# A streaming encoder layer: stick-breaking attention by running sums of logarithms, and by scanned products of sigmoids

## What is computed

```python
def sb_block(q, k, v, q_start):
    z = jnp.einsum('bqhd,bkhd->bhqk', q, k) * scale
    vis = s[None, :] < t[:, None]
    log_keep = jnp.where(vis, jax.nn.log_sigmoid(-z), 0.0)
    later = lax.cumsum(log_keep, axis=3, reverse=True) - log_keep
    w = jnp.where(vis, jnp.exp(jax.nn.log_sigmoid(z) + later), 0.0)
    return jnp.einsum('bhqk,bkhd->bqhd', w, v)

u = a_val * jax.nn.sigmoid(a_gate)
a_out = jax.nn.silu(layernorm(causal_dwconv(concat([conv_hist, u]), conv_w, conv_b), ln_g, ln_b))
b_out = head_rmsnorm(stick_breaking(q, k_all, v_all, q_start), g_sb)
x = x + jnp.concatenate([a_out, b_out], axis=-1) @ w_out
```

## Time and profile before

| | us |
|---|---|
| runs | 595.35, 593.17, 595.15 |
| median | 595.15 |
| the profiled execution, its span from first to last instruction | 594.1 |
| PE busy | 542.8 (91%) |
| DVE busy | 289.6 (49%) |
| ACT busy | 166.8 (28%) |
| GpSimd busy | 105.8 (18%) |

### The profile page before, as it was taken

How to read it: one execution, slowest core, us unless ns; L and a number is a source line. 1 busy time by engine, 2 the same in 40 slices (tenths; PEclk the granted TensorE clock), 3 DMA queues, 4 the chain that set the end, 5 groups by cost and what they waited for, 6 DMA issues and landing times.

```text
span 594.1 us, 7819 instructions
## 1 busy us (share of the span) xinstructions
PE 542.8 (91%) x3097; PEld 330.3 (56%) x3098; DVE 289.6 (49%) x500; ACT 166.8 (28%) x280; POOL 105.8 (18%) x134
## 2 busy tenths in 40 slices
PE   6999999999999999799999799999999878888994
PEld 5779999998766644344554663444443323333331
DVE  2862999998868557362464852111112110011147
ACT  4513123222766776462210201111111111101113
POOL 3100000313431342300101121112112111011003
PEclk9999999999999999799999689999999999889998
DMA  8804745302403600049752879999999999999995
GB/s 294 223 2 148 239 145 172 114 1 57 165 19 89 255 0 1 0 117 421 278 213 88 302 265 400 424 423 424 424 425 417 428 423 422 417 423 421 412 365 171
DMA packets 44763, 148.93 MB, mean 251 GB/s; under 512 B 7124, under 2 KB 23532, under 8 KB 36279
## 3 DMA queue, kind: packets, MB, share of 16 engines
q1 hardware_dynamic: 40263, 139.63, 61.0%
q0 software_dynamic: 4464, 8.80, 3.9%
HBM read 136.29 MB, written 19.59 MB: 262 GB/s over the span
## 4 chain that ended last, share of the span: by engine, by line
PE 62%; DMA 19%; DVE 7%; ACT 4%; SPq 3%; issue 3%; POOL 2%; DVEq 0%; POOLq 0%; ACTq 0%
PE ps L983 17%; DMA big<-in_w_expert_out 12%; PE ps L1211 9%; PE ps L1398 8%; PE ps L1423 5%; DMA cw<-h_dram,low 4%; PE ps L948 3%; PE ps L1095 2%; SPq L642 2%; PE ps L1092 2%; PE ps L1379 2%; DMA y_dram<-cw,low 1%; DVE big L1935 1%; PE ps L1054 1%; PE ps L936 1%
## 5 line engine op out<-in xcount | busy, mean ns | idle before, releaser
L1857 DVE SCALAR_TENSOR_TENSOR big<-low,cwt,big 128x590 f32<-128x590 f32 x120 | 94.2, 841 | 0.4
L2233 DVE TENSOR_TENSOR low<-low,ps 128x256 f32<-128x256 f32 x16 | 6.7, 422 | 172.3 <-ACT low L1706 172.3
L1398 PE MATMUL ps<-big,low 128*64 128x512 f32 x320 | 85.0, 593 | 3.5 <-issue 2.3
L983 PE MATMUL ps<-cw_r 128*128 128x280 f32 x256 | 72.3, 292 | 0.0
L983 PE MATMUL ps<-low_r,cw_r 128*128 128x280 f32 x256 | 72.2, 292 | 0.0
L983 PE MATMUL ps<-cw_r,big_r 128*128 128x280 f32 x256 | 72.1, 291 | 0.0
L1423 PE MATMUL ps<-big,low 128*64 128x512 f32 x160 | 47.0, 630 | 11.7 <-DMA big<-in_w_expert_out 4.8
L1211 PE MATMUL ps<-cw,low 128*128 128x512 f32 x128 | 56.5, 594 | 0.0
L1398 PEld LDWEIGHTS ps<-big,low 128*64 128x64 f32 x320 | 29.8, 137 | 45.7 <-issue 45.7
L983 PEld LDWEIGHTS ps<-cw_r 128*128 128x128 f32 x256 | 47.2, 188 | 0.4 <-issue 0.4
L983 PEld LDWEIGHTS ps<-cw_r,big_r 128*128 128x128 f32 x256 | 47.3, 188 | 0.0
(11 more groups left out here) (285 smaller groups left out, 849.1 us busy)
## 6 DMA issues: line engine op xcount, KB each, us to landing
big<-in_w_expert_in SPq DMA_DIRECT2D x16, 2048.0 KB, 19.8
big<-in_w_expert_out SPq DMA_DIRECT2D x20, 1024.0 KB, 24.3
big<-in_w_in SPq DMA_DIRECT2D x20, 512.0 KB, 5.7
low<-in_w_expert_out SPq DMA_DIRECT2D x8, 1024.0 KB, 30.9
low<-in_w_expert_in SPq DMA_DIRECT2D x4, 2048.0 KB, 23.1
cw<-in_w_expert_in SPq DMA_DIRECT2D x4, 2048.0 KB, 26.8
low<-in_w_expert_in SPq DMA_DIRECT2D x4, 1536.0 KB
big<-in_w_expert_in SPq DMA_DIRECT2D x6, 1024.0 KB, 32.2
```

The lines of the kernel that those rows point to most:

```text
L983: return pe.matmul(ps[:, proj_bank(j) + half, 0:PROJ], w[:, k, :], h[:, k, cols], start=first, stop=last, skip_group_check=True)
L1398: mm = pe.matmul(ps[TILE * half:TILE * half + TILE, gu_bank(g), :], xt[:, k, TILE * half:TILE * half + TILE], wi_at(2 * g + half, k), star ...
L1857: ins = dve.scalar_tensor_tensor(conv[:, i, :], u[:, i, j:j + CW], cwt[:, i, j:j + 1], conv[:, i, :], ALU.mult, ALU.add)
```

## The change

**Attention after.** The list `order` has 24 entries, 21 of them steps, in groups: the four head pairs of query block 0 (128 keys), the few-query units (32 own keys and 512 others for the last prompt positions; 32 own and twice 512 cached keys for the sample), then query blocks 1, 2 and 3 with 256, 384 and 512 keys; three entries that turn the new keys for their output stand between. Queries lie on partitions, keys on columns, and a step holds two heads. Per step:

- PE makes the scores (`scores`). ACT makes two sigmoids of them, of -z (`keeps`) and of z (`betas`), both into SBUF. DVE scans each head's kept fractions from the last key backwards (`running_products`, tensor_tensor_scan, one instruction per head), with both operands the same SBUF tile.
- GpSimd multiplies the betas with the products shifted by one (`weights`), both in SBUF.
- PE turns the weights (`turn_weights`, three entries later), ACT copies them (`copy_weights`), and PE multiplies them with the values (`weigh`, four entries later). A step's score banks come free with `betas` of the step before last.

A group's outputs are copied and squared by ACT (`outputs`), reduced by DVE (`head_means`), rooted by GpSimd, scaled by DVE (`heads_normed`), turned by PE (`turn_out`) and put in place by DVE (`outputs_in`), five to nine entries after the group's end. `weigh` of the first step of a group from block 1 on waits until the group two before is in place.

**The convolution and the LayerNorm.** The first fifteen entries hold two taps each, the later ones none. The LayerNorm as a whole stands behind the attention: mean and variance are eight products each (before: two each, after sums on GpSimd), squares are on ACT. The output projection of chunks 0, 1 and 2 over the attention's channels (`LATE[0:4]`) stands ahead of the mean.

SyncE now waits for the attention's last output ahead of one more weight load, and stores the new keys in three groups. Later stages keep their instructions. The core of the diff:

```diff
-TAPS_STEP = (1, 2, 2, 1, 2, 2, 1, 2, 2, 1, 3, 2, 2, 1, 2, 1, 2, 2, 0, 0, 0, 0, 3)
-MEAN_AT = 26
-LAG = 4
+TAPS_STEP = (2,) * 15
+TURN_LAG, SUM_LAG, OUT_LAG = 3, 4, 5
+MEANS_LAG, ROOT_LAG, NORM_LAG, IN_LAG = 6, 7, 8, 9
...
+        groups = [many(0), few(1, 512, 0, 512) + few(0, S0, 32, PAST), many(1), many(2), many(3)]
+        CHUNK_OF = (0, 4, 1, 2, 3)
+        order = groups[0] + [dict(ko=0)] + groups[1] + [dict(ko=1)] + groups[2] + [dict(ko=2)] + groups[3] + groups[4]
...
+            st["q"], st["bank"] = q, 2 * ((NQ - 1 - q) % 2)
+        for g, sts in enumerate(groups):
+            for n, st in enumerate(sts):
+                st.update(g=g, first=n == 0, last=n == len(sts) - 1)
+        whole = [st for st in steps if "qb" in st]
+        for m, st in enumerate(whole):
+            st.update(left=left[m % 3], before=whole[m - 3] if m >= 3 else None)
...
+            def weights(st):
+
+                s, lo, n = st["s"], st["lo"], st["n"]
+                w = wts[s % 4][:, :, 0:n]
+                pool.wait_ge(beta_ready, s + 1)
+                pool.wait_ge(left_ready, 2 * s + 2)
+                pool.tensor_tensor(w, w, st["left"][:, :, lo + 1:lo + n + 1], ALU.mult).then_inc(w_ready, 1)
+
+            pool.wait_ge(ones_ready, 5)
+            for q in range(NQ + ROOT_LAG):
+                g = group_at(q - ROOT_LAG)
+                if g is not None:
+                    root(stat_o if g == 1 else stat_h)
+                if step_at(q):
+                    weights(step_at(q))
...
                     for a in range(2):
-                        pe.matmul(ps[:, bank + a, 0:st["n"]], kt[64 * a:64 * a + 64, i, P * b:P * b + P],
-                                  qt[64 * a:64 * a + 64, i, P * b:512], start=True, stop=True)
+                        pe.matmul(ps[:, bank + a, 0:n], qt[64 * a:64 * a + 64, i, q0:q0 + P],
+                                  kt[64 * a:64 * a + 64, i, 0:n], start=True, stop=True)
...
+            def turn_weights(st):
+
+                s, n = st["s"], st["n"]
+                pe.wait_ge(w_ready, s + 1)
+                if s:
+                    pe.wait_ge(wtt_ready, s)
+                else:
+                    pe.wait_ge(ckt_ready[0], 2)
+                w = wts[s % 4]
+                for a in range(2):
...
+                    for b in range(n // P):
+                        mm = pe.transpose(ps[:, 4 + a, P * b:P * b + P], w[:, a, P * b:P * b + P], ident[:, :])
+                mm.then_inc(w_turned, 1)
...
             def mean():
-                bank_free(MEAN_AT)
-                pe.wait_ge(ln_summed, NI - 1)
-                for half in range(2):
-                    mm = pe.matmul(ps[:, order[MEAN_AT]["bank"] + half, 0:HALF], nones[:, :], lnt[:, HALF * half:HALF * half + HALF],
-                                   start=True, stop=True)
+                pe.wait_ge(beta_ready, NS)
+                pe.wait_ge(yc_ready, 2 * NI)
+                for i in range(NI):
+                    for half in range(2):
+                        mm = pe.matmul(ps[:, half, 0:HALF], nones[:, :], yc[:, i, HALF * half:HALF * half + HALF],
+                                       start=i == 0, stop=i == NI - 1, skip_group_check=True)
                 mm.then_inc(mean_done, 1)
...
             pe.wait_ge(v_ready, NC + 1)
-            pe.wait_ge(qpair_ready, 1 + 2 * NI)
-            for q in range(NQ + 3):
...
+            for q in range(NQ + SUM_LAG):
                 if q < NQ:
                     if step_at(q):
                         scores(step_at(q))
...
+                if step_at(q - TURN_LAG):
+                    turn_weights(step_at(q - TURN_LAG))
+                if step_at(q - SUM_LAG):
+                    weigh(step_at(q - SUM_LAG))
+                if group_at(q - IN_LAG) is not None:
+                    turn_out(group_at(q - IN_LAG))
+                if q == NQ:
+                    pe.wait_ge(beta_ready, NS - 1)
                     pe.wait_ge(wout_loaded, 16)
-                    project(0, LATE[0:2])
-            pe.wait_ge(w_ready, NS)
-            project(2, LATE[0:2], (0,))
-            head_sums(3)
-            project(2, LATE[0:2], (1,))
-            pe.wait_ge(lnv_ready, 1)
-            project(1, LATE[0:2])
-            project(0, (6,))
-            project(1, (6,))
-            project(0, (7,))
-            project(1, (7,))
+                    project(0, LATE[0:4])
+            for g in range(len(groups)):
+                if group_end[g] + IN_LAG >= NQ + SUM_LAG:
+                    if g == len(groups) - 1:
+                        pe.wait_ge(wtt_ready, NS)
+                        project(1, LATE[0:4])
+                    turn_out(g)
+            pe.wait_ge(mixb_ready, NC)
+            project(2, LATE[0:4])
+            mean()
+            variance()
...
+            def keeps(st):
+                s, n = st["s"], st["n"]
+                act.wait_ge(z_ready, s + 1)
...
+                    act.wait_ge(left_ready, 2 * s - 4)
+                act.activation(keep[s % 3][:, :, 0:n], ps[:, st["bank"]:st["bank"] + 2, 0:n], ACT.Sigmoid, scale=-1.0).then_inc(keep_ready, 1)
+
+            def betas(st):
+                s, n = st["s"], st["n"]
+                if s >= 4:
+                    act.wait_ge(w_turned, s - 3)
+                act.activation(wts[s % 4][:, :, 0:n], ps[:, st["bank"]:st["bank"] + 2, 0:n], ACT.Sigmoid).then_inc(beta_ready, 1)
...
-                act.activation(a, scored(st), ACT.Abs).then_inc(l_chain, 1)
-                act.wait_ge(l_chain, 3 * s + 1)
-                act.activation(a, a, ACT.Exp, scale=-1.0).then_inc(l_chain, 1)
-                act.wait_ge(l_chain, 3 * s + 2)
-                act.activation(a, a, ACT.Ln, bias=1.0).then_inc(l_chain, 1)
...
+            outputs(NC - 1)
+            act.preload_act_table_set("natural_log_exp_and_others")
+            for i in range(NI):
+                deviation_square(i)
             ln_roots()
-            head_roots(2)
-            head_roots(3)
...
-            def softplus(st):
-                s = st["s"]
-                dve.wait_ge(l_chain, 3 * s + 3)
-                if s >= 3:
-                    dve.wait_ge(zr_ready, s - 2)
-                    dve.wait_ge(cs_ready, sums[s - 3])
-                dve.scalar_tensor_tensor(of_step(el[s % 3], st), scored(st), 0.0, of_step(za[s % 2], st),
-                                         ALU.max, ALU.add).then_inc(el_ready, 1)
...
+            def running_products(st):
+
+                s, n, lo, t = st["s"], st["n"], st["lo"], st["left"]
+                dve.wait_ge(keep_ready, s + 1)
+                if "few" in st and not st["own"]:
+                    dve.wait_ge(left_ready, 2 * s)
+                elif st.get("before"):
+                    dve.wait_ge(w_ready, st["before"]["s"] + 1)
+                for a in range(2):
+                    k = keep[s % 3][:, a, 0:n][:, ::-1]
+                    start = t[:, a, lo + n:lo + n + 1] if "few" in st and not st["own"] else 1.0
+                    dve.tensor_tensor_scan(t[:, a, lo:lo + n][:, ::-1], k, k, start, ALU.mult, ALU.min).then_inc(left_ready, 1)
...
+            for q in range(NQ + IN_LAG):
+                if group_at(q - NORM_LAG) is not None:
+                    heads_normed(group_at(q - NORM_LAG))
                 if step_at(q):
-                    softplus(step_at(q))
...
+                    running_products(step_at(q))
+                if group_at(q - MEANS_LAG) is not None:
+                    head_means(group_at(q - MEANS_LAG))
+                if group_at(q - IN_LAG) is not None:
+                    outputs_in(group_at(q - IN_LAG))
                 for _ in range(TAPS_STEP[q] if q < len(TAPS_STEP) else 0):
                     tap(NI)
-                if q == MEAN_AT - 4:
-                    assert not any(taps_left)
-                    first_sum()
-                if q == MEAN_AT:
-                    for i in range(NI):
-                        deviation(i)
-                    heads_normed(0)
-                if q in (MEAN_AT + 2, MEAN_AT + 3):
-                    for i in range(2):
-                        deviation_square(2 * (q - MEAN_AT - 2) + i)
-                if q - 2 == NORM_AT[1]:
-                    heads_normed(1)
+            assert not any(taps_left)
+            for i in range(NI):
+                deviation(i)
             variances()
-            pair_out(3)
-            head_squares(3)
-            heads_normed(2)
             refine()
-            normed(0)
-            normed(1)
-            heads_normed(3)
-            normed(2)
-            normed(3)
+            for i in range(NI):
+                normed(i)
             copy_co(0)
```

More of the change, by code:

```diff
@@ L432, in build @@
             st["s"] = s
-        sums = [sum(not st["last"] for st in steps[:s + 1]) for s in range(NS)]
-        order = list(steps)
-        order.insert(MEAN_AT, dict(ln="mean"))
-        NQ = len(order)
         for q, st in enumerate(order):
-            st["q"], st["bank"] = q, (2, 4, 6)[(NQ - 1 - q) % 3]
```

(59 more changed lines are left out.)

593 lines of the change are left out of this document (234 added, 359 removed).

## The result

The changed kernel takes 615.63 us (median of four runs, 614.07 to 616.49), the kernel before 594.16 in the same comparison: a ratio of 1.0359, with a 95% interval of 1.0319 to 1.0399. It is 3.6% slower; 612 were forecast. The profiled execution has a span of 614.3 us against 594.1.

What follows compares the result with a forecast made beforehand. VectorE and GpSimd's shared SBUF work was taken to bound the attention. The projection's second half starts 15.0 us later, less 3.4 for four products, plus 5 for clock: +16.7, 610.8 profiled, 611.9 median; range 592 to 630.

Steps and rivals of the forecast that it cites:

- the shared pair: Attention steps: VectorE and GpSimd take turns on work with SBUF operands, so both engines' work sums as one resource.
- the LayerNorm's line behind the attention: After the mean: deviations, variance, scaling, ScalarE passes and first Silu follow in one line, formerly hidden; 13.5 us.
- the pair's sum: Attention: scans, products, taps, bias and head scaling on VectorE and GpSimd, 89.4 us together, starting at about 148.5 us.
- the first rival: Attention steps: GpSimd's products run beside VectorE's scans and the kernel gets faster, 586 us; chance .20.
- Prices: Costs taken per operation in the attention: 512-column scan 1.09 us, GpSimd product 2.38 at 1024 columns, tap .75.
- the second rival: VectorE's scans: 512 columns cost .67 us, as a plain pass, giving 601 us; chance .15.
- The tail: TensorE's queue from the last scan: weighings, turns, half projections, mean, 33.9 us, mean done near 275; then LayerNorm, 13.5.
- The clock: TensorE idles twice in the changed tail, before variance and second projection half, and runs slower afterwards: +5 us, bounds 0 and 7.
- The third rival: Attention steps: TensorE falls to 1.2 GHz, a 512 step takes 7.7 us; 624 to 634, taken as 628; chance .12.
- The four products less: Behind the output projection's second half: four products of chunk 2 are moved ahead, -3.4 us.
- One for one to the end: A shift of the output projection's second half reaches the kernel's end in full if weight transfers wait for TensorE.
- K: Start of the output projection's second half: 273.45 us before, forecast 288.5 in the changed kernel, +15.0.

## Why the prediction was right, and where it was not

The sign held, and so did two of the mechanisms, the shared pair and the LayerNorm's line behind the attention; the stall at the key stores was a third that the prediction didn't have. The time came within 3.6 us, partly by luck, because two errors cancelled: the pair's sum was 6.5 us too long, and the stall put 7 us in their place.

- *The pair takes turns.* Right in the main. The rows of 233.66 and 236.13 us show it for scans (1.66 of the product's 2.00 us come on top), and moving the products to VectorE saved 6.9 us where by the first rival it would have cost up to 17. That rival is refuted. The Trainium skill's rule ("SBUF — State Buffer", "SBUF: two separate sides") that one engine holds the shared ports for a whole instruction and the other waits agrees with these rows: 2.76 in place of 2.00 for a product, 6.32 in place of 4.66 for four scans.
- *Prices.* A scan of 512 columns is 1.17 (taken: 1.09; the second rival's .67 is out), of 384 .90, of 256 .63. Products are cheaper than taken: 2.00 at 1024 (2.38), 1.55 at 768 (1.83), 1.09 at 512 (1.28). The two rows from which I went up, .73 at 256 and 1.28 at 512, rise by .55 per 256 columns; measured it is .45. The two errors nearly cancel: by the measured prices the sum is some 88 us in place of 89.4. By half throughput, as the Trainium skill has it ("DVE: opcode table, instruction layouts, handler registers and perf-mode slots", "6. Datapath and trigger behaviour"), a scan was put at 1.34; measured it is 1.17, 1.75 times the plain pass.
- *The end of the last product.* Forecast 241.5, measured 240.12 + 2.00 = 242.1, but by another way. With the stall gone it ends at 235.0, so the sum was 6.5 us too long: 3.5 may be the share of VectorE's other work, if it found room under GpSimd's products altogether, and some of the rest the part of each product that did overlap; neither was measured by itself. The stall put 7 us in their place.
- *The step that failed* is the one on queues. The change moves key stores on SyncE behind a wait and a load, and has the third key copy wait for them on ScalarE; the section on the change names the three groups of stores, and the sum put them at nothing, without a reason. It cost 7.6 us. A wait of this kind is read from the order of one queue: what stands ahead of the transfer that somebody waits for.
- *The tail.* TensorE's list from the last scan to the mean was forecast to end at 275 and ended at 280.13; 4.2 of the 5 are the weighing and the first part of the projection at half clock, .8 a wait for the last outputs ahead of 269.1. The LayerNorm's line was 13.5 and measured 280.15 to 295.06, 14.9, of which 1.9 are the variance at half clock.
- *The clock.* The term was too small: +5 with bounds 0 and 7, and the rows give 1.9 + 2.3 + 1.9 + 2.7 = 8.8. For the two waits that it names the rows give 1.9 + 2.7 = 4.6, so these were priced rightly; the wait ahead of the weighing (236.24 to 240.70) wasn't in it. Nor does each such wait cost the same: ahead of the variance TensorE waited 2.8 us in the kernel after and in the one with the key stores first, and the variance took 5.83 in the one and 4.16 in the other. The third rival came true in its sign only: the clock was .50 from 200 to 220 us, behind the stall, and in these four steps of 384 columns VectorE waited 1.9 to 2.8 us each for the sigmoids; with the stall gone these waits are gone as well and VectorE is full. But the last four steps, of 512 columns, which it priced at 12.6 us, ran at .92 and .93 (220 to 240 us), and up to 10 us more at .50 ahead of them cost 1.4.
- *The four products less*, -3.4, held exactly: from the end of the second part (287.2 and 311.5) to the end of the short chunk (326.4 and 347.3) the lag falls from 24.3 to 20.9.
- *One for one to the end.* Right: a gain at K reached the end, 11.0 + 2.7 in the kernel with the LayerNorm earlier against 13.5 measured.

## What to carry to other kernels

When an operation is moved from one engine to another, ask first whether the two can work at the same time: here VectorE and GpSimd for the most part could not, so the cheapest place for a product was the faster engine, although it was the busy one. Where a tile is used a second time, follow the transfer that frees it through its whole queue; a store behind another's wait is a wait of whoever reuses the tile. And work that can run at any time (a projection's first part, a mean) belongs into the gap where the matrix engine would wait, where it also keeps the clock up.

## What the runs showed of the hardware that was not expected

Small operations wait as well as large ones. VectorE's `tensor_scalar` over 8 columns, with one tensor operand in SBUF, took 1.90 us while a product ran on GpSimd (181.37 in the kernel after), and .17 in the kernel with the products on VectorE:

```profile
177.61 0.65 DVE L1859 TENSOR_REDUCE stat_h<-big 128x8 f32<-128x512 f32 x1
178.30 0.17 DVE L1860 TENSOR_SCALAR stat_h<-stat_h 128x8 f32<-128x8 f32 x1
```

The reduction ahead of it, .65 us, is not lengthened when a product starts beneath it (.65 at 180.68 in the kernel after). GpSimd's root over 8 columns took 2.48 beside scans (228.39) and 1.64 where VectorE was idle (242.22).
